# Fetching an expert's token rows by indirect DMA and storing its results as rows in DRAM, instead of one-hot matmuls

## The reference, cut to what matters

```
logits = (x @ router_w).astype(F32)
top_val, top_idx = lax.top_k(logits, TOP_K)            # TOP_K = 2
top_w = jax.nn.softmax(top_val, axis=-1)
gates = jnp.sum(jax.nn.one_hot(top_idx, N_EXPERTS) * top_w[..., None], axis=-2)
y = jnp.zeros(x.shape, F32)
for e in range(N_EXPERTS):
    y = y + gates[..., e:e + 1] * swiglu(x, w1[e], w3[e], w2[e])
...
def swiglu(x, w1, w3, w2):                             # 1024 -> 3584 -> 1024
    return (jax.nn.silu(x @ w1) * (x @ w3)) @ w2
```

## Time and profile before

| | |
|---|---|
| time, median of 3 runs | 1761.86 us (1761.32 to 1766.3) |
| span of the profiled execution | 1764.4 us |
| its own time | not listed apart; of the three only 1766.3 is above the span, 1.9 us more |
| PE, DVE, ACT, POOL busy | 95%, 74%, 59%, 6% of the span |
| item loop (7 rounds), from the first gather in it to the last | 790.3 to 1560.4 us, six periods of about 128.4 us |
| DMA | 446.78 MB, all issued by SP |

### The profile page before, as it was taken

The page is one execution under the profiler, slowest core; times in us unless marked ns, Lnnn a source line. Parts: engine busy times, 40 slices in busy tenths (PEclk is TensorE's granted clock), DMA queues, the critical chain, the costliest instruction groups (busy, mean ns, idle before and its releaser), DMA issues.

```text
span 1764.4 us, 23971 instructions
## 1 busy us (share of the span) xinstructions
PE 1679.4 (95%) x9050; PEld 1425.9 (81%) x9050; DVE 1310.4 (74%) x1240; ACT 1049.1 (59%) x1012; POOL 102.9 (6%) x95
## 2 busy tenths in 40 slices
PE   6999999999899987999999999999999999999986
PEld 6988789998898866887887887887887887887865
DVE  5976555556696655888888888888888878888864
ACT  5655243335655534766667667666766767677653
POOL 0134100000014310000000000000000000000000
PEclk9999999999999988999999999999999999999998
DMA  7440245455442023997998988988988988988970
GB/s 290 156 143 1 72 144 193 166 215 192 166 169 95 1 95 123 366 367 296 370 337 329 366 333 331 364 339 331 365 332 334 365 327 337 368 328 337 365 296 24
DMA packets 61969, 446.78 MB, mean 253 GB/s; under 512 B 6864, under 2 KB 7248, under 8 KB 7888
## 3 DMA queue, kind: packets, MB, share of 16 engines
q1 hardware_dynamic: 61904, 445.88, 67.0%
HBM read 444.81 MB, written 1.05 MB: 253 GB/s over the span
## 4 chain that ended last, share of the span: by engine, by line
PE 91%; ACT 4%; DVE 3%; issue 1%; POOL 1%; DMA 0%; DVEq 0%; POOLq 0%; ACTq 0%
PE ps L1574 26%; PE ps L1576 26%; PE ps L1575 26%; PE ps L1692 2%; PE ps L1913 2%; DVE wlo L596 2%; PE ps L1982 2%; PE ps L1701 1%; PE ps L1936 1%; ACT whi L592 1%; PE ps L1761 1%; ACT xh L950 1%; PE ps L1690 1%; PE ps L1562 1%; POOL work L717 1%
## 5 line engine op out<-in xcount | busy, mean ns | idle before, releaser
L596 DVE TENSOR_TENSOR wlo<-raw,whi 128x2048 fp32r<-128x2048 f32 x421 | 943.7, 2288 | 114.8 <-ACT whi L592 114.8
L592 ACT CAST whi<-raw 128x2048 fp32r<-128x2048 f32 x421 | 782.3, 1916 | 36.9 <-DMA raw<-in_experts 36.5
L1574 PE MATMUL ps<-whi,xh 128*128 128x512 f32 (+3 forms) x1568 | 623.9, 398 | 31.0 <-DVE wlo L596 19.2
L1575 PE MATMUL ps<-wlo,xh 128*128 128x512 f32 (+3 forms) x1568 | 616.5, 393 | 0.0
L1576 PE MATMUL ps<-whi,xl 128*128 128x512 f32 (+3 forms) x1568 | 616.5, 393 | 0.0
L1574 PEld LDWEIGHTS ps<-whi,xh 128*128 128x128 f32 x1568 | 298.2, 190 | 98.3 <-DVE wlo L596 15.2
L1576 PEld LDWEIGHTS ps<-whi,xl 128*128 128x128 f32 x1568 | 297.9, 190 | 66.7
L1575 PEld LDWEIGHTS ps<-wlo,xh 128*128 128x128 f32 x1568 | 298.4, 190 | 63.5
L1574 PE MATMUL ps<-xh,whi 128*128 128x256 f32 x656 | 186.4, 284 | 0.0
L1575 PE MATMUL ps<-xl,whi 128*128 128x256 f32 x656 | 184.9, 282 | 0.0
L1576 PE MATMUL ps<-xh,wlo 128*128 128x256 f32 x656 | 184.9, 282 | 0.0
(11 more groups left out here) (239 smaller groups left out, 1345.9 us busy)
## 6 DMA issues: line engine op xcount, KB each, us to landing
raw<-in_experts SPq DMA_DIRECT2D x336, 1024.0 KB, 4.8
raw<-in_stream SPq DMA_DIRECT2D x85, 1024.0 KB, 4.8
cst<-in_consts SPq DMA_DIRECT2D x1, 1382.5 KB, 13.3
h<-in_x SPq DMA_DIRECT2D x1, 1024.0 KB, 4.8
out<-work SPq DMA_DIRECT2D x2, 512.0 KB, 2.7
work<-in_final_w SPq DMA_DIRECT2D x1, 512.0 KB, 5.8
rws<-in_rows SPq DMA_DIRECT2D x1, 204.0 KB, 4.4
cols<-in_columns SPq DMA_DIRECT2D x1, 92.0 KB, 4.3
```

The costliest lines, as they stand in the source:

```text
L592: nc.scalar.copy(whi[:, n % RING, :], raw[:, n % RING, :]).then_inc(s_hi, 1)
L596: nc.vector.tensor_tensor(wlo[:, n % RING, :], raw[:, n % RING, :], whi[:, n % RING, :].bitcast(F32), ALU.subtract).then_inc(s_lo, 1)
L1574: pe.matmul(out, ah, bh, start=start, stop=False)
L1575: pe.matmul(out, ah, bl, start=False, stop=False)
```

## The change

For the first item nothing changes in the gather: DVE makes `pick` and PE multiplies. For all others:

- POOL writes the normalised tokens `hn` to DRAM once (`x_rows`). DVE works out for every token and each of its two experts the item and the place in it (`row_numbers`, 26 small instructions, placed behind the table and before the first item's `gathered` on DVE). POOL scatters the token numbers to a DRAM table by four indirect DMAs of 128 words and reads the table back (`slots`).
- In each round POOL fetches the 128 rows of the next item by an indirect DMA into `xg` (the first block of `hn`), and PE turns them with 8 transposes in place of the 16 matmuls.
- ACT still copies the item's result to `ysb`. POOL then writes it to DRAM (`y_rows`, 512 KB). The four matmuls, the four adds, the two transposes of `pickg` and the second instruction of each selection leave the round.
- After the loop POOL fetches each token's rows from `y_rows` by four indirect DMAs of 512 KB (`earlier_results`), and DVE adds each times its gate to `h` during blocks 2 to 5 of the last item. The last item itself still goes back by `pickg`, transposes and matmuls, all within that item.
- Before, during the dense part of layer 0, POOL zeroes the table, row 0 of `y_rows` and the rows of possible second items (2.6 MB written).

```
@@ PE
+            def gather(it):
+                pe.wait_ge(s_xg, through(16, it, 16))
+                for half in range(2):
+                    key = ("GA", "each", half)
+                    opened(key, it)
+                    for q in range(4):
+                        k = 4 * half + q
+                        ins = pe.transpose(bank(key, P * q, P), xg[:, P * k:P * k + P], ident)
+                    ins.then_inc(s_fill, 1)
...
                 if ph == "each":
                     up("B", ph, 0, it)
-                drained(pe, ("GT", "each"), "a", it, 1)
+                    return
+                drained(pe, ("GT",), "a", it)
@@ POOL
+            def item_rows(it):
+                filled(pool, ("GA", "each", 1), it, 1)
+                nc.gpsimd.tensor_copy(now_token[:, :], slot_token[:, bass.ds(it + 1, 1)])
+                pool.drain()
+                pool.indirect_dma_start(xg, None, x_rows, bass.IndirectOffsetOnAxis(ap=now_token[:, 0:1], axis=0)).then_inc(
+                    s_xg, 16)
+            def item_results(it):
+                drained(pool, ("YY", "each", 1), "a", it)
+                pool.dma_start(y_rows[bass.ds(it * P + 1, P), :], ysb).then_inc(s_yw, 16)
+                pool.wait_ge(s_yw, it * 16 + 32)
+            def earlier_results():
+                for n in range(NB * TOPK):
+                    pool.indirect_dma_start(yg[n], None, y_rows,
+                                            bass.IndirectOffsetOnAxis(ap=to_y[:, n:n + 1], axis=0)).then_inc(s_yg[n], 16)
...
             rstd(1)
+            zeros()
             rstd(2)
             mixers(1)
             rstd(4)
+            for who in "av":
+                pool.wait_ge(s_hn[who], 5)
+            pool.dma_start(x_rows.rearrange("(b p) c -> p b c", p=P), hn[:, :, :]).then_inc(s_xrow, 16)
+            slots()
+            pool.wait_ge(s_xrow, 16)
+            filled(pool, ("GA", "first", 1))
+            pool.wait_ge(s_tab, 1)
+            items = pool.value_load(table[0:1, MORE + 3:MORE + 4], min_val=NE - 1, max_val=NE - 1 + MORE)
+            with pool.Fori(0, items) as i:
+                item_rows(i)
+                item_results(i)
+            earlier_results()
@@ ACT
+                act.wait_ge(s_yw, through(16, it, 16))
                 for m in range(2):
                     filled(act, ("YY", ph, m), it)
                     nc.scalar.copy(ysb[:, 512 * m:512 * m + 512], bank(("YY", ph, m))).then_inc(s_free["a"], 1)
                 if ph == "each":
                     split.behind(("YY", ph, 1), it)
-                    scatter_matrix(ph, it)
                     split.behind(("B", ph, 0), it)
@@ DVE
+            def earlier_result(n):
+                dve.wait_ge(s_yg[n], 16)
+                v = h[:, n % NB, :]
+                nc.vector.scalar_tensor_tensor(out=v, in0=yg[n], scalar=row_gate[:, n:n + 1], in1=v, op0=ALU.mult,
+                                               op1=ALU.add).then_inc(st.sem, st.up())
...
+                    if ph == "last" and 2 <= j < 2 + NB * TOPK:
+                        if j == 4:
+                            step()
+                        earlier_result(j - 2)
...
-                for m in range(2):
-                    for b in range(NB):
-                        add_to_residual(("SC", ph, b, m), b, m, it)
                 if ph == "each":
                     split.behind(("B", ph, 0), it)
+                else:
+                    step()
+                    for m in range(2):
+                        for b in range(NB):
+                            add_to_residual(("SC", b, m), b, m, it)
...
             with dve.Fori(0, items) as i:
-                filled(dve, ("GT", "each"), i, 1)
-                selection(i + 1)
                 rest_of_item("each", i)
             split.after()
+            last_selection(items)
             rest_of_item("last", items)
```

More of the change, by code:

```diff
@@ L204, in round_tiles @@
         t.add(("TT", ph, j - 1), 6 + (j - 1) % 2, "av")
-        if j == NJ - 1 and not last:
-            gather_tiles(t, ph)
+        if j == NJ - 1:
+            if last:
+                t.add(("GT",), 2, "a")
+            else:
+                gather_tiles(t, ph)
         t.add(("B", ph, j), 2 * (j % 2) + 1, "v")
@@ L214, in round_tiles @@
         t.add(("B", ph, 0), 1, "v")
[L215 to L218, removed]
+    if last:
+        for m, b, bank in ((0, 0, 2), (0, 1, 6), (1, 0, 7), (1, 1, 3)):
+            t.add(("SC", b, m), bank, "v")
 def plan_tiles():
@@ L952, in gathered, with scatter_matrix @@
                     ins.then_inc(s_free["a"], 1)
-            def scatter_matrix(when, it):
-                filled(act, ("GT", when), it)
-                nc.scalar.copy(back, bank(("GT", when), 0, T)).then_inc(s_free["a"], 1)
+            def scatter_matrix(it):
+                filled(act, ("GT",), it)
+                nc.scalar.copy(back, bank(("GT",), 0, T)).then_inc(s_free["a"], 1)
             def silu(ph, j, it):
@@ L1385, in _, with first_selection @@
             split.behind(("WO", 1, 1, 1))
-            def selection(i):
+            def first_selection():
                 for b in range(NB):
[L1390 to L1393, removed]
+                    ins = nc.vector.tensor_scalar(pick[:, b, :], cc("slots"), posi[:, b, 0:1], None, ALU.is_equal)
@@ L1903, in _, with first_gather @@
             ins.then_inc(s_fill, 1)
-            def gather(when, it, number):
-                pe.wait_ge(s_pick, number)
+            def first_gather():
+                pe.wait_ge(s_pick, 1)
                 for half in range(2):
-                    key = ("GA", when, half)
-                    opened(key, it)
+                    key = ("GA", "first", half)
+                    opened(key)
                     for q in range(4):
@@ L1964, in rest_of_item @@
                     turn(ph, j - 1, it)
-                    if j == NJ - 1 and ph == "each":
-                        gather(ph, it, it + 2)
+                    if j == NJ - 1:
+                        if ph == "each":
+                            gather(it)
+                        else:
+                            scatter_matrix(it)
                     up("B", ph, j, it)
@@ L1980, in rest_of_item @@
                     for b in range(NB):
-                        opened(("SC", ph, b, m), it)
-                        pe.matmul(bank(("SC", ph, b, m)), back[:, P * b:P * b + P], ysb[:, 512 * m:512 * m + 512], start=True,
+                        opened(("SC", b, m), it)
+                        pe.matmul(bank(("SC", b, m)), back[:, P * b:P * b + P], ysb[:, 512 * m:512 * m + 512], start=True,
                                   stop=True).then_inc(s_fill, 1)
-                if ph == "each":
-                    scatter_matrix(ph, it)
-            gather("first", None, 1)
+            first_gather()
             drained(pe, ("GA", "first", 1), "v")
             up("A", "first", 0, None)
-            scatter_matrix("first", None)
             up("B", "first", 0, None)
```

117 lines of the change are left out of this document (106 added, 11 removed).

## The result

| | before | after |
|---|---|---|
| time, median | 1764.08 us (1761.32 to 1767.0, 4 runs) | 1723.6 us (1718.88 to 1724.83, 4 runs) |
| ratio after/before, 95% interval | | 0.9762 [0.9745, 0.9779] |
| span of the profiled execution | 1764.4 us | 1720.8 us |
| its own time | | 1722.51 us |

The forecast was 1717.5 us (1711 to 1735). The medians differ by 40.5 us, the two profiled spans by 43.6 us, where 44.3 was forecast. The forecast counts from the span of the profile, so the 43.6 us are what its terms have to be held against.

The account below looks back on a forecast made before the run. The prediction took PE's instruction stream plus a 0.5 us stall per round as the bound. 44.5 + 0.3 + 0.2 - 0.2 - 0.5 = 44.3 us off the 1761.9 us median gave 1717.6, rounded to 1717.5 us (range 1711 to 1735).

Parts of the forecast that it names:

- What bounds the kernel: Item loop: a round is PE's instruction stream plus one 0.5 us stall, so work taken off PE saves its full length.
- The gather and the scatter: Each of seven rounds: gather saves 2.70 us, scatter 3.65 us, together 6.35 us, 44.5 us in all.
- The stall stays: Each round, behind B(6): PE's wait for DVE's split stays 0.5 us; gone entirely, it would be worth another 3.5 us.
- Transfers hidden, taken as 0: Each round: POOL's write and fetch delay loads by 2.4 to 2.9 us, at no cost to PE; high end 20 us.
- cushion: Item loop: how late a load may land before PE waits, worked out as 4.9 us.
- `row_numbers` nearly all hidden: Before the first item: 3.7 us on DVE, nearly all hidden by ACT's drain; 0.2 us lost, PE gaining 0.3 us net.
- The last item: Last item: four fetches and the last write, 6 us of DMA, cost 0 to 1 us once, taken as 0.5.
- Rival 1: Blocks 0 and 1, after POOL's write: late loads cost 1 to 3 us a round, time 1724 to 1738; chance 0.12.
- Rival 2: Rounds: DVE waits for POOL's copy and DMA preparations, 3 us a round, 10 us in all, time 1728; chance 0.06.
- Rival 3: Rounds: DMA ceiling for loads mixed with writes; at 358 GB/s a 126 us round, 17 us saved, time 1745; chance 0.05.
- Rival 4: Rounds: POOL's row transfers make loads late beyond cushion and saving, slower from 12 us; at 16 us, 1795; chance 0.03.
- Rival 5: Rounds: PE's freed time turns at once into waits for DVE's splits, no gain, time 1762; chance 0.02.

Follow-up runs that it names:

- `gather_only`: Changed kernel with only the gather by fetched rows; the scatter stays with matmuls and nothing is stored; 1745.69 us, ratio 0.9894 to before.
- `scatter_only`: Changed kernel with only the results stored as DRAM rows; every item is still gathered by matmuls; 1737.88 us, ratio 0.9849 to before.
- second pair of profiles: Both kernels run again unchanged: before 1766.55 us (span 1764.7), after 1721.91 us (span 1720.2).
- `split_first`: Changed kernel with the last item's four fetches spread over its blocks and one load split ahead of the gathered copies; 1715.09 us, again 1716.16 us.
- `no_transfers`: Changed kernel without POOL's fetch and write in each round, PE turning the same rows every time; 1718.84 us, ratio 0.9751 to before.
- `fetch_x5`: Changed kernel with the same 128 rows fetched four times more in each round, into idle buffers; 1728.23 us, one run.
- `row_numbers_twice`: Changed kernel with 23 of the 26 small instructions of `row_numbers` done twice; 1723.88 us, one run.
- `after_again`: Changed kernel run once more, unchanged; 1721.91 us, ratio 0.977 to before.
- `fetch_x2`: Changed kernel with the same 128 rows fetched once more in each round, into an idle buffer; 1718.62 us, one run.

## Why the prediction was right, point by point

1. **What bounds the kernel: right.** A round was read as PE's stream plus 0.5 us. Taking work off PE shortened the round by 6.16 us of a forecast 6.35. `gather_only` and `scatter_only` show each part on the path by itself.
2. **The gather and the scatter: right in price.** The transposes cost the 0.88 us worked out from the turn. The 0.19 us a round that is missing, 1.3 us over seven, is not in these prices. The sum took the pitch of the other matmuls as the same before and after; it was 232.9 ns in before's loop and 233.3 in after's. With that counted out, the parts and the whole come to 2.69, 3.65 and 6.33 us against the 2.70, 3.65 and 6.35 worked out (below). In the second pair of profiles the rounds are 128.36 and 122.07 us, 6.29 less.
3. **The stall stays: right.** 0.5 us in the earlier trace rows and in after. `split_first` shows its cause, the order of drain and split, and that 0.4 us of it could be had.
4. **Transfers hidden, taken as 0: right.** This was the step with the greatest risk. The lateness was 3.1 us, where 2.4 to 2.9 was worked out from bytes, and the cushion 4.7 to 4.9, where 4.9 was worked out. `no_transfers` has the same round and `fetch_x5` finds the edge. That 3.1 came so near to the bytes is partly luck: one transfer alone, 1.2 to 1.4 us by its bytes, made loads 1.9 to 2.8 us late (below), and a further fetch added 1.0. The upper bound for the fetch itself was too low. It lands 9.7 us after its issue (median of seven), not at most 4.8. The index list alone is not the reason. In `gather_only`, where the same fetch has no write ahead of it and is issued right behind the gather, it lands after 4.0 to 4.5 us in each of the six rounds (the 6.1 is the one ahead of the loop):

```profile
DMA to landing us min/median/max: 4.0/4.3/6.1
```

   In after it comes right behind the write, while the weights' loads are late themselves. It cost nothing, because PE wants the rows some 80 us later.
5. **`row_numbers` nearly all hidden: right.** 3.0 us, not 3.7, and DVE ready with ACT, so PE lost nothing where 0.2 us was allowed. `row_numbers_twice` shows that in the profiled after it was the last 3 us that could be hidden there.
6. **The last item: under-sized.** 1.6 us for the four fetches (1.0 in `after_again`), where 0.5 was taken from a range of 0 to 1. The working had the right sum, DMA time against the cushion. It counted 6 us of DMA for the four fetches and the write, and the loads came 6.5 us late. With a seventh round of 6.16, this stretch comes out as 6.16 - 0.2 - 1.6 - 0.6 = 3.8 us, the table's figure; the 0.6 us are the clock at the end (8.4 us for 24 matmuls in after, 7.8 in before).
7. **The rivals.** Rival 1 (loads late at a cost in each round): the loads are late, but it costs nothing; `fetch_x5` is what it looks like when it is true. Rival 2 (POOL and DVE): DVE's splits took 2288 ns in the mean before and 2289 after. POOL was the one that waited, once:

```profile
1185.44 2.33 POOL L780 COPY now_token<-slot_token 128x1 int32 x1 [5.59 <-DMA y_rows<-work]
```

   The same copy takes 0.18 us in the other rounds. DVE in that moment:

```profile
1185.44 4.49 DVE L626 TENSOR_TENSOR wlo<-raw,whi 128x2048 fp32r<-128x2048 f32 x2
```

   The first of these two splits ended at 1187.72 and the copy at 1187.77. That agrees with the earlier trace rows. It is the same in all kernels: 27 of 63 such copies fell into a split, and each ended 0.04 to 0.05 us behind it. None of this reached PE. Rival 3 (a ceiling of DMA): 369 GB/s over a whole round and 406 over 30 us, with a round of 122.2 and not 126. The Trainium skill's figure of about 358 GB/s ("DMA: Bandwidth & Descriptors", Specifications) is passed by these rows. Rival 4 (slower): its condition was 12 us of lateness; it was 3.1. Rival 5 (the gain turns into waits for splits): 0.5 us of them, as before.

Of the 6.1 us by which the median of 1723.6 us lies above the forecast, 0.7 us are in the span (1720.8 for 1720.1). The other 5.4 us are in the step from span to median. I took the forecast median 2.5 us below the span, because before's profiled span was 2.5 us above the median of its first three runs. But the time of every execution is 1.7 to 2.1 us above its own span, so before's profiled execution was the slowest of those three (only 1766.3 fits its span of 1764.4), while after's (1722.51) is 1.1 us below its median. A profiled execution is one of a scatter of some 5 us, and the distance that it happens to have from the median carries over to no other kernel. That 1723.6 lies within the stated range doesn't depend on this step; how near the forecast comes does. The narrower range of the forecast's own mechanism, 1712 to 1723, was missed by 0.6 us, and rival 1 begins at 1724; what decides between the two is the round of 122.20 us and `no_transfers`, not the median.

## What to carry to other kernels

Take the bound from one round of the steady state. If it is one engine's instruction stream, work moved off it is worth its own length, and prices from pitches of neighbours in the trace hold to some hundredths of a microsecond, once the pitch of the unchanged work is compared too: 0.2% more of it hid 0.2 us of each round's gain here. Whether the traffic that replaces it is hidden is a question of how late one load may land, not of the mean busy share: work out that cushion from one load's way through the engines, compare it with the largest burst, and look for the place where several bursts fall together. Here that was not the loop but the four fetches behind it.

## What the runs showed of the hardware

- **DMA share.** 0.97 at 364 GB/s looked full, and 1.00 came with 406 GB/s and 1.04 with 438. From 364 to 438 GB/s the bytes grow by a fifth and the share by 7%, so a value near 1 doesn't say that nothing more goes in.
- **Indirect DMA.** In after's loop 128 rows of 4 KB landed 7.4 to 9.9 us after the issue, behind the write and beside a stream of 1 MB loads, and in `gather_only`'s loop 4.0 to 4.5 us. Several in a row queue: the four of the last item landed after 8.8, 10.0, 11.6 and 14.1 us. The issue held POOL for 0.9 to 3.1 us. Either transfer alone made the loads beside it late by much the same: at worst 2.2 to 2.8 us in a round of `gather_only` (the fetch) and 1.9 to 2.6 in one of `scatter_only` (the write), against up to 3.1 for both in after.
- **Writes.** POOL's write of 512 KB landed in 5.2 us beside the loads; SP's of that size took 2.7, but at the end of the kernel, with no loads beside it. POOL's write of 1 MB (`x_rows`) landed in 4.4 us while no load was under way. So the 5.2 us can't be put down to POOL's queue.
- **VectorE and GpSimd.** A POOL copy of 0.18 us that falls into a DVE split of 2.29 us ends 0.04 to 0.05 us after it, 27 times out of 27, and the splits keep their 2.29.
- **Two rhythms of matmuls.** In after the starts of the 128x512 matmuls lie 0.229 and 0.238 us apart in turn, 2.800 us for twelve. In other kernels and in some rounds of the same kernel they go through 0.241, 0.233, 0.231, 0.231, 0.229, 0.230, 0.232 us, 2.789 for twelve. A block of 72 takes 16.88 or 16.82 us. `after_again` has rounds of both kinds (start, us, what, its chain):

```profile
789.85 0.87 PE ps L2067 x8
...
912.02 0.87 PE ps L2067 x8
...
1033.86 0.87 PE ps L2067 x8
```

  That is 122.17 us and 121.84 us for the same instructions. The matmuls' starts can be counted. A round wholly at the slow rhythm has 245 distances of 0.237 or 0.238 us, one wholly at the quick rhythm none, and `fetch_x2` has both kinds, 0.37 us apart. Over the loop the share of the slow rhythm is 0.52 in before, 0.98 in after, 0 in `gather_only`, 0.12 in `scatter_only` and 0.02 in `split_first`. Taking 0.37 us times that share off each kernel's round leaves these savings:

  | | measured | at one rhythm | worked out before |
  |---|---|---|---|
  | gather alone | 2.88 | 2.69 | 2.70 |
  | scatter alone | 3.80 | 3.65 | 3.65 |
  | whole change | 6.16 | 6.33 | 6.35 |

  So the rhythm accounts for the 6.16 us in place of 6.35, and for the 0.5 us between the sum of the two parts and the whole. What chooses the rhythm stays open; no run here was made to set it.
